# Stick-breaking attention: the value products of even and odd query chunks in two PSUM banks instead of one

## The reference, cut to what matters

```python
def stick_breaking_mix(q, k, v):
    """A[t,s] = sigmoid(z_ts) * prod_{s<j<t} (1 - sigmoid(z_tj)), strictly causal (s < t)."""
    for blk in range(T // SB_BLOCK):            # 8 blocks of 128 queries
        z = jnp.einsum('bthd,bshd->bhts', qb, kp).astype(jnp.float32) * scale
        causal = jnp.arange(t1)[None, :] < jnp.arange(t0, t1)[:, None]
        log_1mb = jnp.where(causal, -jax.nn.softplus(z), 0.0)
        rem = lax.cumsum(log_1mb, axis=3, reverse=True) - log_1mb
        a = jnp.where(causal, jnp.exp(jax.nn.log_sigmoid(z) + rem), 0.0)
        outs.append(jnp.einsum('bhts,bshd->bthd', a.astype(v.dtype), vp))
```

## Time and profile before

| | us |
|---|---|
| median of 3 runs | 2967.72 |
| lowest and highest run | 2965.39 and 2972.66 |
| profiled execution | 2988.82 |
| its span, first to last instruction | 2987.5 |
| TensorE busy in the span | 2875.9 |
| DVE busy | 1858.2 |
| ACT busy | 1204.7 |

### The profile page before, as it was taken

How to read it: one execution, slowest core, us unless ns; L and a number is a source line. 1 busy time by engine, 2 the same in 40 slices (tenths; PEclk the granted TensorE clock), 3 DMA queues, 4 the chain that set the end, 5 groups by cost and what they waited for, 6 DMA issues and landing times.

```text
span 2987.5 us, 36065 instructions
## 1 busy us (share of the span) xinstructions
PE 2875.9 (96%) x14312; PEld 2407.0 (81%) x14312; DVE 1858.2 (62%) x2615; ACT 1204.7 (40%) x1810; POOL 68.9 (2%) x44
## 2 busy tenths in 40 slices
PE   8999999999999999999999977899999999999998
PEld 6888878887788888888778856788887888888887
DVE  4148766625766666666641277577457777777774
ACT  3144454634433323334331265776433333333432
POOL 0002210010000000000000000000000000000000
PEclk9999997999999999999999988888999999999999
DMA  4111220032211111113121100000211111111122
GB/s 169 50 36 57 79 99 1 6 123 78 106 56 50 51 57 52 50 54 127 50 92 57 37 14 10 22 1 1 92 43 42 50 57 57 47 53 57 56 93 85
DMA packets 47831, 172.99 MB, mean 58 GB/s; under 512 B 5648, under 2 KB 6160, under 8 KB 47664
## 3 DMA queue, kind: packets, MB, share of 16 engines
q1 hardware_dynamic: 47664, 170.68, 17.1%
HBM read 145.23 MB, written 25.43 MB: 57 GB/s over the span
## 4 chain that ended last, share of the span: by engine, by line
PE 87%; DVE 8%; ACT 3%; issue 2%; DMA 0%; SPq 0%; DVEq 0%; ACTq 0%
PE PS L295 14%; PE PS L297 14%; PE PS L299 14%; PE PS L1598 8%; PE PS L1599 8%; PE PS L1600 8%; PE PS L483 2%; PE PS L485 2%; PE PS L484 2%; PE PS L1186 2%; PE PS L706 2%; PE PS L1156 1%; PE PS L1171 1%; PE PS L3118 1%; DVE H L2790 1%
## 5 line engine op out<-in xcount | busy, mean ns | idle before, releaser
L289 DVE TENSOR_TENSOR w_lo<-w_raw,w_hi 128x1024 fp32r<-128x1024 f32 x93 | 117.1, 1262 | 203.1 <-ACT w_hi L283 203.1
L1598 PE MATMUL PS<-u_hi_f,w_hi 128*128 128x512 f32 x624 | 242.7, 389 | 0.0
L1599 PE MATMUL PS<-u_lo_f,w_hi 128*128 128x512 f32 x624 | 242.7, 389 | 0.0
L1600 PE MATMUL PS<-u_hi_f,w_lo 128*128 128x512 f32 x624 | 242.7, 389 | 0.0
L1547 ACT ACTIVATE w_hi<-weight_sums 128x512 fp32r<-128x512 f32 x156 | 98.1, 629 | 356.0 <-DVE weight_sums L1568 197.1
L283 ACT ACTIVATE w_hi<-w_raw 128x1024 fp32r<-128x1024 f32 x93 | 97.6, 1054 | 263.4 <-PE PS L485 136.5
L295 PE MATMUL PS<-f_ah,w_hi 128*128 128x512 f32 x640 | 197.1, 389 | 0.1
L297 PE MATMUL PS<-f_al,w_hi 128*128 128x512 f32 x640 | 197.0, 389 | 0.0
L299 PE MATMUL PS<-f_ah,w_lo 128*128 128x512 f32 x640 | 197.0, 389 | 0.0
L1553 DVE TENSOR_TENSOR w_lo<-w_raw,w_hi 128x512 fp32r<-128x512 f32 x205 | 137.3, 688 | 92.9 <-ACT w_hi L1547 92.9
L1598 PE MATMUL PS<-f_T_hi,w_hi 128*128 128x512 f32 x468 | 182.8, 390 | 1.9 <-issue 1.9
(11 more groups left out here) (447 smaller groups left out, 6612.4 us busy)
## 6 DMA issues: line engine op xcount, KB each, us to landing
w_raw<-in_weights SPq DMA_DIRECT2D x215, 512.0 KB, 3.6
H<-in_x_t SPq DMA_DIRECT2D x16, 512.0 KB, 4.3
h_kept<-H SPq DMA_DIRECT2D x16, 512.0 KB, 5.1
H<-h_kept SPq DMA_DIRECT2D x16, 512.0 KB, 6.7
stick_kept<-stick_stage SPq DMA_DIRECT2D x12, 512.0 KB, 2.8
mixer<-stick_kept SPq DMA_DIRECT2D x9, 512.0 KB, 6.8
p_kept<-p_stage SPq DMA_DIRECT2D x8, 512.0 KB, 4.0
p_pp<-p_kept SPq DMA_DIRECT2D x8, 512.0 KB, 8.1
```

Of the source, the lines that this page charges most:

```text
L289: dve.tensor_tensor(self.w_lo[i][:], self.w_raw[i][:], self.w_hi[i][:].bitcast(F32), ALU.subtract).then_inc(*self.s("w_lo").up(g))
L1598: pe.matmul(out, hi[:, self.chunk(k)], rh, start=opens and k == 0, stop=False, skip_group_check=True)
L1599: pe.matmul(out, hi[:, self.chunk(k)], rl, start=False, stop=False, skip_group_check=True)
L1600: mm = pe.matmul(out, lo[:, self.chunk(k)], rh, start=False, stop=k == 3, skip_group_check=True)
```

## The change

The sum of query chunk t goes to bank 7 for even t and to bank 6 for odd t. A value product that opens query chunk t then waits for the put of t-2, and no longer of t-1. Bank 7 is also where the next pair's value steps are transposed, so two waits are added on TensorE. The transposes of step 10 also wait for the put of t = 4. The value product that opens t = 6 also waits for ACT's copy of the second half of the next pair's values. Both are there for the pairs that have a next pair, three times each.

```diff
+    def stick_bank(self, t):
+        return 7 - t % 2
+
@@ pe_stick_prepare
         pe.wait_ge(*self.s("sb_value_steps").at(pair))
+        if pair:
+            pe.wait_ge(*self.s("sb_put").at((pair - 1) * TT + 4))
@@ pe_stick
-                if opens and pair * TT + t:
-                    pe.wait_ge(*self.s("sb_put").at(pair * TT + t - 1))
-                values = self.stick_values(pair)
+                if opens and pair * TT + t >= 2:
+                    pe.wait_ge(*self.s("sb_put").at(pair * TT + t - 2))
+                if opens and t == 6 and pair + 1 < PAIRS:
+                    pe.wait_ge(*self.s("sb_values").at(pair + 1, 1))
+                values, bank = self.stick_values(pair), self.stick_bank(t)
...
-                        mm = pe.matmul(self.PS[:, 6, hh * SB_DH:(hh + 1) * SB_DH], self.sb_at[n % 2][:, hh, self.chunk(b)],
+                        mm = pe.matmul(self.PS[:, bank, hh * SB_DH:(hh + 1) * SB_DH], self.sb_at[n % 2][:, hh, self.chunk(b)],
@@ dve_stick
-                dve.tensor_copy(H[:, 4 + pair, t * P:(t + 1) * P], self.PS[:, 6, 0:P]).then_inc(
+                dve.tensor_copy(H[:, 4 + pair, t * P:(t + 1) * P], self.PS[:, self.stick_bank(t), 0:P]).then_inc(
```

## The result

The changed kernel is slower: 2977.06 us median of 12 runs against 2967.07 us of 12 runs of the kernel before. The ratio is 1.0038, with a 95% interval of 1.0026 to 1.0051. (It is the ratio on record for these runs taken beside each other; the quotient of the two medians is 1.0034.) Forecast was 2967.7 us and no change.

A forecast was written before the change was run, and what follows sets the result against it. The prediction took TensorE, busy 2875.9 of 2987.5 us, to bound the kernel. Its terms, -1.99 + 2.01 + 0 + 0 = 0.0 us, left the median at 2967.7 us, with a range of 2950 to 2985 us.

The forecast's parts named there:

- Term 1: Step 10 of pair 0: piece 6's value product no longer waits idle for the put of t = 4; -1.99 us.
- Term 2: Step 10 of pair 0: the next pair's value-step transposes still wait for DVE, so idle time moves behind the product; +2.01 us.
- 30 of the 31 waits cost nothing: Of 31 relaxed waits for a put, 30 showed no TensorE idle time before, so relaxing them is worth 0.
- The added waits: Step-10 transposes on the put of t = 4, and t = 6's opening product on ACT's copy: cost 0, at most 1.8 us.
- Pairs 1 to 3: The interval between piece 6's value products of pairs 1 and 2 was to stay at 36.95 us.
- Against it: the gap doesn't shrink.: Pair 0, 453.12 to 456.2 us: same 2.0 us idle and 1.1 us product in exchanged order, so the clock stays alike.
- clock, for the worse: Rival: the gap behind the thin product brings TensorE's clock down where before it did not; +17.4 us, 2985.1 us, chance 0.14.
- The base: Profiled execution of 2988.8 us, 21.1 above the runs' median; the forecast carried over the difference to 2967.7 us, not the level.
- the sum: All terms together: -1.99 + 2.01 + 0 + 0 = 0.0 us, with ends of -2.0 and +1.8; no change, chance 0.60.
- the two clock cases: TensorE's clock fall in pair 0 avoided (2950.3 us, chance 0.15) or newly met (2985.1 us, chance 0.14); they set the range.

The follow-up runs named there:

- one_relaxed: Kernel before with two banks and the added waits; only piece 6's value product in pair 0 waits for the put of t-2; 2974.56 us, ratio 1.0019.
- before_third_look: The kernel before, unchanged, run again for a trace of a usual execution; 2964.70 us.
- two_banks_old_waits: Changed kernel with its two banks and added waits, but every opening value product waits for the put of t-1 as before; 2966.38 us, ratio 0.9988.
- after_gate_later: Changed kernel with DVE's gating half steps moved out of pair 0, to every third step from 12 on; 2967.23 us, ratio 0.9991.
- after_dense_behind: Changed kernel with its gap left and 8 useless 512-column matmuls behind it, ahead of piece 7's value product; 2975.31 us, ratio 1.0003.
- after_look_2: The changed kernel, unchanged, run again for a further trace; 2973.82 us.
- after_look_3: The changed kernel, unchanged, run once more for a further trace; 2988.91 us.
- before_filled_gap: Kernel before with 8 useless 512-column matmuls in the gap ahead of piece 6's value product in pair 0; 2968.58 us, ratio 0.9999.
- after_filled_gap: Changed kernel with 8 useless matmuls in its gap, between piece 6's value product and the value-step transposes; 2970.79 us, ratio 1.0002.
- both gate_later: Kernel before and changed kernel, each with DVE's gating moved out of pair 0; 2968.31 us, ratio 0.9996, and 2967.23 us, ratio 0.9991.
- filled_plus_11: before_filled_gap with 11 more useless 512-column matmuls on TensorE in pair 1; 2973.06 us, ratio 1.0006.
- filled_plus_21: before_filled_gap with 21 more useless 512-column matmuls on TensorE in pair 1; 2972.37 us, ratio 1.0007.
- before_longer_gap: Kernel before with an extra DVE memset ahead of the put of t = 4 in pair 0, lengthening the gap in its old place; 2969.39 us, ratio 0.9999.
- before_look_4: The kernel before, unchanged, run once more for a further trace; 2973.10 us.
- all_relaxed_but_one: Changed kernel, but piece 6's value product in pair 0 (t = 5) waits for the put of t = 4 as before; 2972.63 us, ratio 1.0017.

## Why the prediction was wrong, point by point

**The put's wait goes, the value steps' wait comes in its place (terms 1 and 2).** Right in kind. Term 1 was right: the product starts behind the transposes without a wait. Term 2 was mis-sized: 2.01 us were forecast, and 2.49, 2.48 and 2.24 us measured in the changed kernel's two usual traces and in one_relaxed. The first half of the difference, 0.25 us, is in all three. I had put the product's 1.08 us behind a pause; behind other matmuls it takes 1.00 and its start overlaps theirs, so it ends 0.83 us behind the transposes. The other half, 0.24 us, is only where the other 30 waits are relaxed too. So it isn't true that 30 of the 31 waits cost nothing. The opening product of t = 3 in pair 0 was held up a little, and the rows of idle time don't show it. First before_third_look, then the changed kernel:

```profile
441.16 0.42 PE L1171 MATMUL PS<-ident,sb_rem 128*128 128x128 f32 x2
441.58 1.97 PE L1186 MATMUL PS<-mixer_rows,sb_at 128*128 128x64 f32 x16
```

```profile
440.81 0.41 PE L1176 MATMUL PS<-ident,sb_rem 128*128 128x128 f32 x2
441.05 1.90 PE L1193 MATMUL PS<-mixer_rows,sb_at 128*128 128x64 f32 x16
```

DVE's put of t = 2 starts at 441.17 and at 440.81 us. Counted from it, the product ends at 2.38 us before and at 2.14 after. TensorE reaches piece 6 that much earlier, DVE does not, and the gap grows. By itself the whole mis-sizing is worth less than 0.5 us.

**The added waits.** Right: cost 0. The copy ended at 502.27 us and the product started at 503.21 in pair 1, 0.94 us to spare, as before. two_banks_old_waits has both added waits and both banks at 2966.4 us. So the rule of the Trainium skill, "Perfetto Trace Analysis", section "Matmuls", on rotating banks bought nothing in this kernel: the one put that TensorE could be seen to wait for was followed by a later wait. The two traces with the gating moved agree with the rule, with 2.8 us in pairs 1 to 3.

**Pairs 1 to 3.** Right: from the product of piece 6 in pair 1 to that in pair 2 it is 533.12 - 496.16 = 36.96 us in the changed kernel, where 36.95 were forecast. From the first to the last start of their value products it is 585.2 - 479.3 = 105.9 us in the changed kernel and 580.8 - 475.0 = 105.8 in before_third_look.

**"Against it: the gap doesn't shrink."** This is the step that failed: that exchanging the gap and the thin product leaves the clock alone, since the stretch holds the same idle time and the same work. The clock falls near the end of the gap in both kernels. In the kernel before's two usual traces it is low for only 3.4 us (before_third_look below), then back. In the changed kernel's two it stays down for 13.7 and 13.6 us.

```profile
454.00:456.00 2.00, 2.00 (x10) 0.51 0.00 0
456.00:458.00 2.00, 2.00 (x14) 0.64 0.01 4
458.00:460.00 2.00, 2.00 (x21) 1.00 0.00 0
```

(13.7 - 3.4) us at half speed are 5.1 us, near the 4.7 us that pair 0 grew. That the gap is the cause is shown by filling it in the changed kernel and by taking it away (after_gate_later), and one trace of after_dense_behind speaks for it that the work behind the gap has a part in how long the clock stays down. The Trainium skill, "TensorE: Matmul & The Clock Gate", section "What's actually happening", says that activity releases the low clock. The traces agree in part: the clock came back earlier when the work was denser, but in the changed kernel TensorE was fully busy by the profile for over 10 us and stayed at 1.2 GHz. That most of the loss of the usual executions comes with this one relaxed wait is shown by one_relaxed against two_banks_old_waits. Why a gap of 2.2 to 2.5 us is worse behind the product than ahead of it is not shown. One thing differs between the traces. In the changed kernel's two usual ones the fall began 0.5 and 0.6 us before the gap ended; in the others that have the gap and a fall, of either kernel and of the experiments, it began 0.3 to 2.3 us behind its end (worked out from 2 us windows as above). What that decides was not tested.

**The rival "clock, for the worse"** is the one that came true, with a chance of 0.14 given to it. Its place was right (the gap at step 10 of pair 0), and so was the guess that usual executions do without the long fall of the earlier trace rows. Its price was not: 17.4 us was set for the fall in the 2989 executions, which has 37.5 us at the low clock. The changed kernel usually pays 4.7. Even for the long fall the price was a little high. From the product of piece 6 in pair 0 to that in pair 1 a usual execution of the kernel before takes 491.79 - 453.29 = 38.50 us and not 36.95, so the long fall cost 54.37 - 38.50 = 15.9 us there. The long fall was no state of the changed kernel alone: the kernel before has it in 15 of 149 executions (the 12 beside the changed kernel counted too), the changed one in 4 of 14, after_look_2 and after_look_3 included. With the gap filled or gone (before_filled_gap, after_filled_gap, both gate_later, filled_plus_11 and filled_plus_21) it came in 0 of 72. But it came in 0 of 23 too in before_longer_gap and after_dense_behind, which have the gap, so whether the gap stands does not alone decide it. Whether the change makes it more frequent can't be said from 14 executions.

**The base.** The profiled execution belonged to the rare kind. I carried a difference over and noted the 21 us, but took the fall at 457 to 494 us as part of the kernel's usual course when I argued that nothing would change. That the measured 2977.1 us lies inside the range of 2950 to 2985 us is no merit of the sum: the range had been stretched to the two clock cases.

**What stays open.** The usual executions differ by about 9 us in their medians (2976.2 against 2967.1), and 4.7 us are placed. The rest is not placed. The later attention stage has two lengths, 4.3 us apart, in both kernels, and whether the changed kernel meets the long one more often, two usual traces of each can't tell. The times give a hint: at 2971 to 2975 us, where before_look_4 lies with the long form, are 17 of 149 executions of the kernel before, but 5 of 12 of all_relaxed_but_one and 6 of 12 of after_filled_gap, which both keep the other relaxed waits. Neither group has a trace, so a part of the loss may come from those waits in a way that is not shown.

## What to carry to other kernels

Before a wait is relaxed, look at what stands between it and the next wait on the same engine: here the idle time only moved behind the product. Two banks pay only where a put is late. On TensorE it also matters where idle time stands and what work follows it: here the clock came back after 3.4 us with eight wide matmuls behind the gap (one trace) and after 13.6 to 13.7 us without. Where one profiled execution is 0.7% above the median of the runs, take more traces before arguing from it.

## What the runs showed of the hardware

- With eight useless matmuls in a gap of 2 to 2.5 us the clock was 2.4 GHz from 440 us to the end of pair 0 in three of four traces, of both kernels. In the fourth (filled_plus_11) it was low for 3.4 us behind another idle time. None of the 48 executions of these four kernels was at 2989 us.
- TensorE can be busy without a pause and keep 1.2 GHz, for 13 us in the changed kernel's usual trace and for 37.5 us in the executions at 2989 us.
- An untouched stage takes 148.2 to 148.6 us or 152.5 to 152.7 us with the same instructions, in all traces of this case but one (149.5), with other falls of the clock in it. Two executions of one kernel can differ by 8 us in this way and another (2964.7 and 2973.1 us).
- Delays don't add up in the total: 2.4 us more work on TensorE cost 4.5 us over before_filled_gap, and 4.6 us more cost 3.8, measured on another chip, where the kernel before was itself 1.1 us slower.
